# Reordering the delta network's convolution, and loading expert 0's weights before the router has chosen

## The chip, the cores and the metric

The kernel runs on one core of a Trainium2 chip. The metric is the device time of one execution in microseconds (us). A core has a matrix engine (TensorE, PE in the rows, with its weight loads as PEld), a vector engine (DVE), a scalar engine (ACT), a general engine (GpSimd, POOL) and a sync engine (SP), each with an instruction stream of its own that runs strictly in order. They wait for each other through semaphores. SP computes nothing; it issues most DMAs. SBUF is the on-chip memory, PSUM holds the matrix products in eight banks.

## The reference, cut to what matters

Two transformer blocks of depth 1 over 1024 tokens with 1024 features, one after the other, all in float32. Only the first block is touched by the change:

```python
h = modulate(rmsnorm(x, norm1_w), shift1, scale1)
r_q, r_k, r_v, r_g, d_q, d_k, d_v, d_z, d_a, d_b = split(h @ w_in)
ret = rmsnorm(retention(rotary(r_q), rotary(r_k), r_v)) * silu(r_g)
cq, ck, cv = split(silu(causal_dwconv(concat(d_q, d_k, d_v), conv_w)))   # 4 taps, 12 groups of 128 channels
dq, dk = l2norm(cq) * DN_HEAD_DIM ** -0.5, l2norm(ck)
beta, g = sigmoid(d_b), -exp(a_log) * softplus(d_a + dt_bias)
dn = rmsnorm(gated_delta_rule(dq, dk, cv, g, beta)) * silu(d_z)
x = x + gate1 * (concat(ret, dn) @ w_out)                                # the residual stage
h2 = modulate(rmsnorm(x, norm2_w), shift2, scale2)
# router: best of 4 groups, then best 2 of its 8 experts; 32 experts of 1024 -> 512 -> 1024
hid = silu(ragged_dot(xs, w1)) * ragged_dot(xs, w3)
x = x + gate2 * segment_sum(ragged_dot(hid, w2) * gate)
```

The second block (neighbourhood attention with a bias table `rpb`, gated linear attention, a 4096-wide MLP) reads the bias table that the convolution stage prepares on the side.

## The kernel before, in words

The program is a chain of stages, each ended by a barrier (`k.meet()`: every engine, SP too, announces itself and waits for the last one): `front` (modulation and the first projections), `retention`, `delta_conv`, `delta`, `residual`, `route`, `experts_pass`, and the second block's stages.

**The convolution stage** (`delta_conv`, 365 to 550 us) projects the 12 groups of channels in 6 pairs, `p` = 0 to 5. A pair is 7 steps of 4 matmuls (a Strassen-like scheme on sums of weights and sums of tokens). Step `n` writes a PSUM bank that step `n - 2` used, so it waits for what takes step `n - 2` out of the bank (`conv_taken`). Steps 0, 2, 3 and 6 are taken out by ACT (`conv_copy_scalar`, line 1380), steps 1, 4 and 5 by DVE (`conv_add_vector`, line 1462). After a pair, DVE applies the 4 taps (`conv_taps_vector`, lines 1479 and 1483), ACT the SiLU (line 1387), TensorE turns the channels into token rows between the steps of the next pair (`delta_conv_turn`, helper line 232), ACT and DVE take those out, and GpSimd scales them (`conv_rows_gpsimd`). Also on GpSimd: the sums of weights (`conv_weights_gpsimd` 1505 to 1511, `conv_last_weights_gpsimd` 1519), and the window mask that is added to the bias table of the second block (`near_bias_gpsimd`, line 1232, four adds of 128 x 960).

At the stage's start each stream does the gates too: TensorE turns `abT` (1289), DVE takes it out (1418), and ACT makes sigmoid, exp, abs, exp, ln (1338 to 1347) before it enters the pair loop. At its end, `delta_ahead` runs four steps of the delta stage's first tile on each engine before the barrier: on TensorE inside the last turn (1302), on GpSimd before the last group's rows (1545), on ACT and DVE after everything else.

**The residual stage** stores the rows of `x` and of its normed form `xn` from SP (1916, 1918), and SP waits for these stores before the barrier (1919 to 1921).

**The experts stage.** The router sorts 2048 token-expert pairs into blocks of up to 128 rows of one expert (or two half blocks of two experts, line 2526). `known` is the semaphore value that says the list of blocks is there. SP then loads weights, 6.3 MB for an expert as three DMAs of 2 MB (`experts_load`, 2427, 2428, 2435), into three sets of buffers in turn. A load into a set in use waits until TensorE is through with it. GpSimd gathers the blocks' token rows by indirect DMA (2462) once the tokens of each block are known. TensorE's first block waits for the first gather, the turned rows and the weights. With these inputs the router gives expert 0 84 of the 2048 pairs, and each expert with over 64 has a whole block of its own, so the first block is expert 0's.

## Time and profile before

| what | value |
|---|---|
| median of 3 runs | 3084.66 us (3079.02 to 3085.67) |
| the profiled execution | 3084.89 us, its span 3083.1 us |
| mean granted TensorE clock | 0.97 of full |
| TensorE busy | 2899.4 us (94%), 12002 matmuls |
| DVE, ACT, POOL busy | 39%, 20%, 23% |
| convolution stage, by the trace | 365 to 550 us |
| TensorE's first expert matmul, the last | 977.97 us, 1539 us |
| DMA | 415.12 MB, mean 135 GB/s; 403 to 426 GB/s from 1002 us to 1387 us |

The time is that of the whole program, and TensorE is busy for nearly all of it. What can be won is where TensorE waits. The profile's views give that by stage: the waits of one engine in a window, the instructions of each engine in order of time with the idle time ahead of them and what ended it, and the share of the DMA engines in short windows. A row's duration is of the whole merged group when it has "x" and a count. A busy share hides what matters here: two engines can be busy and slow each other down.

### The profile page before, as it was taken

The numbers are of one execution on the slowest core, as the hardware profiler recorded it, in microseconds if no ns is written. First come the engines' busy times: TensorE is split into PE (matmuls) and PEld (weight loads), VectorE is DVE, ScalarE is ACT, GpSimd is POOL, SyncE is SP. The second block draws the span as 40 slices with busy tenths as digits, with TensorE's granted clock in tenths as the row PEclk, the third lists the DMA queues.
The fourth block names the chain that finished last, engine by engine and source line by source line (L and its number), as shares of the span: only waits on it lengthen the run. The fifth ranks groups of instructions, "written<-read, shape, count | busy, mean of one in ns | idle before, by whom it ended". The sixth has DMA issues, their size and how long they took to land.

```text
span 3083.1 us, 30795 instructions
## 1 busy us (share of the span) xinstructions
PE 2899.4 (94%) x12002; PEld 1723.0 (56%) x12002; DVE 1209.6 (39%) x1999; ACT 629.7 (20%) x1351; POOL 714.1 (23%) x552
## 2 busy tenths in 40 slices
PE   7999899889897999999969999999999999999998
PEld 5786544788544666666634455557544444444443
DVE  6714766466213111111134134569734314133142
ACT  4001222322121221211222211147231000000001
POOL 3213455544121000000021000137521122111220
PEclk9999999899998999999989999999999999999999
DMA  8634486000216999999671100030201111111101
GB/s 263 221 55 51 92 193 171 1 28 28 90 77 269 403 426 425 426 426 407 269 257 62 55 1 14 14 106 1 85 32 55 41 41 41 41 55 42 41 28 55
DMA packets 180120, 415.12 MB, mean 135 GB/s; under 512 B 30644, under 2 KB 103796, under 8 KB 170872
## 3 DMA queue, kind: packets, MB, share of 16 engines
q1 hardware_dynamic: 163545, 370.52, 34.0%
q10 hardware_dynamic: 10512, 25.69, 2.6%
q0 software_dynamic: 5904, 16.78, 1.5%
q8 instruction: 100, 1.64, 0.2%
q14 instruction: 59, 0.48, 0.0%
HBM read 366.04 MB, written 59.88 MB: 138 GB/s over the span
## 4 chain that ended last, share of the span: by engine, by line
PE 87%; DVE 6%; issue 2%; DMA 2%; ACT 1%; POOL 1%; SPq 0%; DVEq 0%; ACTq 0%; POOLq 0%
PE bank L3760 27%; PE bank L2523 9%; PE bank L2526 8%; PE bank L2953 5%; PE bank L748 4%; PE bank L1267 4%; PE bank L1935 4%; PE bank L3127 3%; PE bank L232 3%; PE bank L3125 2%; PE bank L3459 2%; PE bank L883 2%; PE bank L3469 2%; PE bank L1838 1%; PE bank L1835 1%
## 5 line engine op out<-in xcount | busy, mean ns | idle before, releaser
L3760 PE MATMUL bank<-w_ff,uT 128*128 128x512 f32 x640 | 276.0, 592 | 0.0
L3760 PE MATMUL bank<-hT,w_ff 128*128 128x512 f32 x512 | 224.3, 596 | 4.3 <-DVE hT L3563 4.3
L3883 DVE TENSOR_TENSOR x_out<-x_out,bank 128x512 f32<-128x512 f32 x140 | 94.7, 687 | 291.5 <-PE bank L3760 291.3
L3760 PEld LDWEIGHTS bank<-w_ff,uT 128*128 128x128 f32 x640 | 121.6, 190 | 153.1 <-issue 153.1
L2523 PE MATMUL bank<-e_w,e_xsT 128*128 128x256 f32 x832 | 185.0, 383 | 1.6 <-DVE e_xsT L2609 1.6
L2526 PE MATMUL bank<-e_w,e_xsT 128*64 128x256 f32 x1408 | 159.3, 386 | 18.7 <-issue 18.7
L2523 PEld LDWEIGHTS bank<-e_w,e_xsT 128*128 128x128 f32 x832 | 158.6, 192 | 32.7 <-issue 11.3
L2953 PE MATMUL bank<-w_gla,nT 128*128 128x512 f32 x384 | 168.5, 599 | 1.3 <-ACT nT L2915 1.3
L3760 PEld LDWEIGHTS bank<-hT,w_ff 128*128 128x128 f32 x512 | 97.5, 191 | 126.3 <-issue 126.1
L3760 PE MATMUL bank<-h_sum,w_ff 128*128 128x512 f32 x384 | 166.1, 592 | 0.0
L2680 DVE TENSOR_TENSOR e_hid<-e_act,bank 128x256 f32<-128x256 f32 x48 | 20.2, 421 | 337.1 <-PE bank L2523 171.1
L2526 PEld LDWEIGHTS bank<-e_w,e_xsT 128*64 128x64 f32 x1408 | 113.1, 139 | 68.6 <-issue 30.2
L3824 POOL TENSOR_TENSOR w_ff<-w_ff,w_ff 128x2048 f32<-128x2048 f32 x9 | 42.7, 4749 | 355.7 <-PE bank L3760 352.5
L2953 PEld LDWEIGHTS bank<-w_gla,nT 128*128 128x128 f32 x384 | 73.2, 192 | 91.8 <-issue 89.4
L3760 PEld LDWEIGHTS bank<-h_sum,w_ff 128*128 128x128 f32 x384 | 73.0, 190 | 91.8 <-issue 91.8
L3797 ACT ACTIVATE uT<-bank 128x512 f32<-128x512 f32 x48 | 28.3, 600 | 468.9 <-PE bank L3760 468.9
L3870 DVE TENSOR_TENSOR uT<-uT,bank 128x512 f32<-128x512 f32 x48 | 33.1, 689 | 229.1 <-PE bank L3760 229.0
L3127 PE MATMUL bank<-nT,w_nqk 128*128 128x512 f32 x256 | 121.7, 605 | 0.0
L2462 POOL DMA_INDIRECT e_rows<-xn_rows,e_idx x25 | 25.0, 1001 | 405.1 <-PE bank L2492 402.6
L748 PE MATMUL bank<-w_in,hT 128*128 128x256 f32 x512 | 115.2, 383 | 0.0
L3444 POOL TENSOR_SCALAR n_sc<-n_sc,n_st 128x512 f32<-128x512 f32 x64 | 99.7, 1563 | 46.9 <-DVE n_st L3427 44.7
L3760 PE MATMUL bank<-w_ff,u_sum 128*128 128x512 f32 x256 | 110.5, 592 | 0.0
(534 smaller groups left out, 4932.9 us busy)
## 6 DMA issues: line engine op xcount, KB each, us to landing
e_w<-in_w SPq DMA_DIRECT2D x105, 2048.0 KB, 28.5
w_ff<-in_w_ff SPq DMA_DIRECT2D x32, 1024.0 KB, 5.3
y_rows<-zero SPq DMA_DIRECT2D x8, 3008.0 KB, 20.5
wa_rest<-in_w_ada SPq DMA_DIRECT2D x32, 512.0 KB, 6.0
y_rows<-e_y ACTq DMA_DIRECT2D x24, 512.0 KB, 10.1
wa<-in_w_ada SPq DMA_DIRECT2D x16, 512.0 KB, 11.0
w_qkv<-in_w_in SPq DMA_DIRECT2D x24, 256.0 KB, 8.4
w_gla<-in_w_in SPq DMA_DIRECT2D x3, 2048.0 KB, 20.3
```

The source lines that it names most:

```text
L232: t = k.nc.tensor.transpose(bank[:, h * P:(h + 1) * P], src[:, h * P:(h + 1) * P], k.c("ident"))
L748: t = pe.matmul(out, still[:, f, g * P:(g + 1) * P], moving[:, f, :], start=step in (0, 1, 3) and g % 2 == f == 0, stop=f == 3, skip_group ...
L883: t = pe.matmul(k.bank[6 + m % 2][:, :], hT[:, f, m * P:(m + 1) * P], wz[:, f, :], start=f == 0, stop=f == NK - 1)
L1267: t = pe.matmul(conv_bank(k, p, step)[:, :], weights[step][:, f, :], tokens[step](f), start=step in (0, 1, 3) and f == 0, stop=f == 3, ski ...
L1935: t = pe.matmul(k.bank[2 * (m % 2) + h][:, :], mixed, b.w[h][:, f, :], start=f == 0, stop=f == NK - 1)
L2523: return pe.matmul(out, xT, weights[0], start=start, stop=stop)
L2526: t = pe.matmul(out[tokens, :], xT[:, tokens], w, start=start, stop=stop)
L2953: t = pe.matmul(k.bank[3 * (i % 2) + j][:, :], b.nT[:, f, i * P:(i + 1) * P], b.w[at][:, f, :], start=f == 0, stop=f == NK - 1)
L3127: t = pe.matmul(bank[:, :], wqk[c // 2 % 2][:, f, c % 2 * P:(c % 2 + 1) * P], nT[:, f, h * BANK:(h + 1) * BANK], start=f == 0, stop=f == N ...
L3444: g.tensor_scalar(b.sc[n][:, :], b.sc[n][:, :], b.st[n][:, 2:3], None, ALU.mult).then_inc(*s.weights_ready.up().inc)
L3760: t = pe.matmul(bank[:, :], still, moving, start=step in (0, 1, 3) and f == 0, stop=f == 3, skip_group_check=True)
L3883: v.tensor_tensor(dst, dst, k.bank[4 * ((ph + step) % 2) + g][:, :], ALU.add).then_inc(*s.added.up().inc)
```

## The change

Five edits reorder the convolution stage, and one moves a load.

1. ACT's gate chain (sigmoid to ln) moves from before the pair loop to behind the copy of step 0 (`conv_gates_scalar`).
2. DVE's add of step 1 of pair 0 moves ahead of the gates.
3. GpSimd's four mask adds, once together behind group 2's rows, come one by one at the end of the rounds `p` = 1 to 4.
4. TensorE's four ahead steps move from inside the last turn to before the turns of the last two groups.
5. GpSimd's ahead steps move from before the last group to before the last two.
6. SP loads expert 0's three matrices into the set at 96 KB at the end of the residual stage, before its barrier. The sets are renumbered, so that this one is the first. After `known`, the first block's loads are skipped if its expert is 0 (a DMA with a condition), and done again otherwise.

```diff
-def near_bias_gpsimd(k, s, b):
+def near_bias_gpsimd(k, s, b, p):
...
-    for p in range(PAIRS):
-        b3 = b.bias[:, p, :].rearrange("p (r c) -> p r c", c=W)
-        g.tensor_tensor(b3, b3, wide(k.c("window"), 1, 2 * KH - 1), ALU.add).then_inc(*s.bias_ready.up().inc)
+    b3 = b.bias[:, p, :].rearrange("p (r c) -> p r c", c=W)
+    g.tensor_tensor(b3, b3, wide(k.c("window"), 1, 2 * KH - 1), ALU.add).then_inc(*s.bias_ready.up().inc)
@@ delta_conv_tensor
+    pe.wait_ge(*conv_taken(s, CONV_PAIRS - 2, 5))
+    pe.wait_ge(*conv_taken(s, CONV_PAIRS - 2, 6))
+    pe.wait_ge(*s.rows_ready(2 * RH))
+    delta_ahead(ahead)
     for j in (LAST_CHANNELS - 1, LAST_CHANNELS):
-        delta_conv_turn(k, s, b, j, ahead)
+        delta_conv_turn(k, s, b, j)
@@ delta_conv_scalar
-    a.wait_ge(*s.ab_taken(2))
-    a.activation(d.beta[:, :, :], b.ab[:, :, RH:], ACT.Sigmoid).then_inc(*s.beta_ready.up().inc)
...
         if p < CONV_PAIRS:
             conv_copy_scalar(k, s, b, p, 0)
+        if p == 0:
+            conv_gates_scalar(k, s, b, d)
@@ delta_conv_vector
     v.tensor_tensor(a21, a11, a21, ALU.subtract).then_inc(*s.x_summed.up().inc)
+    conv_add_vector(k, s, b, 0, 1)
     v.wait_ge(*s.ab_turned(1))
...
-        if p < CONV_PAIRS:
+        if 0 < p < CONV_PAIRS:
             conv_add_vector(k, s, b, p, 1)
@@ conv_rows_gpsimd
-        if j == 2:
-            near_bias_gpsimd(k, s, b)
...
-    if j == LAST_CHANNELS:
-        g.wait_ge(*conv_made(s, CONV_PAIRS - 1, 6))
-        g.wait_ge(*s.rows_ready(2 * RH))
-        g.wait_ge(*s.g_ready(1))
-        delta_ahead(ahead)
@@ delta_conv_gpsimd
+        if p == CONV_PAIRS:
+            g.wait_ge(*conv_made(s, CONV_PAIRS - 1, 6))
+            g.wait_ge(*s.rows_ready(2 * RH))
+            g.wait_ge(*s.g_ready(1))
+            delta_ahead(ahead)
         if p:
             for j in (2 * p - 2, 2 * p - 1):
-                conv_rows_gpsimd(k, s, b, dtok, d, j, ahead)
+                conv_rows_gpsimd(k, s, b, dtok, d, j)
+        if 1 <= p <= PAIRS:
+            near_bias_gpsimd(k, s, b, p - 1)
@@ residual_sync
         sy.wait_ge(*(s.xn_stored_0, s.xn_stored_1)[n](NT // 2))
+    for j in range(3):
+        experts_first_load(k, s, sets, j)
@@ experts_first_load, experts_sync, experts_load
+def experts_first_load(k, s, sets, j):
+
+    k.nc.sync.dma_start(sets[0][j][:, :, :], experts_source(k.io, j, slice(0, 1))).then_inc(*s.first_set_got.up().inc)
...
     sy.wait_ge(*known)
+    sy.wait_ge(*first_got)
     used = used_blocks(sy, experts)
...
+    if u == 0:
+        there = which[0] > 0
```

How the streams read before and after. First ACT at the start of the convolution stage (`abT` is the raw gates, `gates_u` and `alog` the gate chain, `conv_raw` the copies of steps 0, 2, 3). Before:

```order
L1336 ACTIVATE abT_120<-bank 8x512 x2
L1338 ACT_TABLE_LOAD
L1338 ACTIVATE beta_135<-ab_124 128x32
L1340 ACT_TABLE_LOAD
L1340 ACTIVATE alog_125<-alog_125 128x4
L1343 ACTIVATE gates_u_1_129<-gates_u_1_128 128x32
L1345 ACTIVATE gates_u_1_129<-gates_u_1_129 128x32
L1347 ACT_TABLE_LOAD
L1347 ACTIVATE gates_u_1_129<-gates_u_1_129 128x32
L1380 ACTIVATE conv_raw_1_116<-bank 128x512
L1380 ACTIVATE conv_raw_1_115<-bank 128x512 x2
```

After:

```order
L1334 ACTIVATE abT_120<-bank 8x512 x2
L1385 ACTIVATE conv_raw_1_116<-bank 128x512
L1367 ACT_TABLE_LOAD
L1367 ACTIVATE beta_135<-ab_124 128x32
L1369 ACT_TABLE_LOAD
L1369 ACTIVATE alog_125<-alog_125 128x4
L1372 ACTIVATE gates_u_1_129<-gates_u_1_128 128x32
L1374 ACTIVATE gates_u_1_129<-gates_u_1_129 128x32
L1376 ACT_TABLE_LOAD
L1376 ACTIVATE gates_u_1_129<-gates_u_1_129 128x32
L1385 ACTIVATE conv_raw_1_115<-bank 128x512 x2
```

The copy of step 0 is now ahead of the gates, the copies of steps 2 and 3 are still behind them.

GpSimd in the middle of the stage, from the scaling of group 2's rows on (`conv_ss` is the square sums of a group, `dtok` its rows). Before:

```order
L1536 TENSOR_TENSOR dtok_60<-dtok_60,conv_ss_123 128x8x128
L1232 TENSOR_TENSOR near_bias_131<-near_bias_131,consts_49 128x960 x4
L239 TENSOR_SCALAR conv_ss_123<-conv_ss_123 128x8
L241 TENSOR_TENSOR conv_ss_123<-conv_ss_123,consts_49 128x8
L1532 TENSOR_SCALAR conv_ss_123<-conv_ss_123 128x8
L1536 TENSOR_TENSOR dtok_60<-dtok_60,conv_ss_123 128x8x128
L1519 TENSOR_TENSOR w_qkv_1_1_105<-w_qkv_1_1_105,w_sum_1_109 128x512
```

After, the same stretch:

```order
L1542 TENSOR_TENSOR dtok_60<-dtok_60,conv_ss_123 128x8x128
L239 TENSOR_SCALAR conv_ss_123<-conv_ss_123 128x8
L241 TENSOR_TENSOR conv_ss_123<-conv_ss_123,consts_49 128x8
L1538 TENSOR_SCALAR conv_ss_123<-conv_ss_123 128x8
L1542 TENSOR_TENSOR dtok_60<-dtok_60,conv_ss_123 128x8x128
L1231 TENSOR_TENSOR near_bias_131<-near_bias_131,consts_49 128x960
L1525 TENSOR_TENSOR w_qkv_1_1_105<-w_qkv_1_1_105,w_sum_1_109 128x512
```

One of four mask adds is left here, behind both groups' rows.

TensorE at the end of the stage (`conv_out_1_117` is group 10, `conv_out_1_118` group 11; line 1797, later 1803, and the `dtok` turns are the ahead steps). Before:

```order
L1267 MATMUL bank<-hT_52,w_qkv_1_1_105 128x512 x4
L232 MATMUL bank<-consts_49,conv_out_1_117 128x128 x8
L232 MATMUL bank<-consts_49,conv_out_1_118 128x128 x4
L1797 MATMUL bank<-hT_52,consts_49 128x512
L232 MATMUL bank<-consts_49,dtok_60 128x128 x4
L232 MATMUL bank<-consts_49,conv_out_1_118 128x128 x4
L232 MATMUL bank<-consts_49,dtok_60 128x128 x4
```

After:

```order
L1266 MATMUL bank<-hT_52,w_qkv_1_1_105 128x512 x4
L1803 MATMUL bank<-hT_52,consts_49 128x512
L232 MATMUL bank<-consts_49,dtok_60 128x128 x4
L232 MATMUL bank<-consts_49,conv_out_1_117 128x128 x8
L232 MATMUL bank<-consts_49,conv_out_1_118 128x128 x8
L232 MATMUL bank<-consts_49,dtok_60 128x128 x4
```

The ahead steps stand before all turns of the last two groups.

## Rows read from the trace of the kernel before

**Rows 1.** TensorE's waits, 360 to 560 us: us in total, times, longest
```profile
PE bank L1267 <- ACT conv_raw L1380: 7.0, 1, 7.0
PE bank L1267 <- DVE conv_raw L1462: 4.1, 1, 4.1
```

**Rows 2.** Timeline, stage start: start, us, instruction, count [idle before]
```profile
369.85 3.70 PE L1267 MATMUL bank<-hT,w_qkv 128*128 128x512 f32 x8
380.51 9.25 PE L1267 MATMUL bank<-dtok,w_sum 128*128 128x512 f32 x16 [6.97 <-ACT conv_raw L1380]
396.47 10.46 PE L1267 MATMUL bank<-hT,w_qkv 128*128 128x512 f32 x24
...
372.50 3.35 DVE L1414 TENSOR_TENSOR hT<-hT 128x2048 f32<-128x2048 f32 x1
376.94 5.69 DVE L1425 TENSOR_TENSOR h_last<-hT,dtok 128x512 f32<-128x512 f32 x4
...
370.50 3.19 POOL L1511 TENSOR_TENSOR w_sum<-w_qkv,w_qkv 128x512 f32<-128x512 f32 x1
```

**Rows 3.** Timeline, middle of the stage: TensorE, DVE, GpSimd
```profile
467.31 5.09 PE L1267 MATMUL bank<-dtok,w_sum 128*128 128x512 f32 x8 [4.05 <-DVE conv_raw L1462]
494.58 3.60 PE L1267 MATMUL bank<-dtok,w_sum 128*128 128x512 f32 x8
...
397.46 0.75 DVE L1479 TENSOR_SCALAR conv_out<-conv_raw,conv_w 128x1024 f32<-128x1024 f32 x1
402.88 3.93 DVE L1483 SCALAR_TENSOR_TENSOR conv_out<-conv_raw,conv_w,conv_out 128x1024 f32<-128x1024 f32 x3
449.55 0.75 DVE L1479 TENSOR_SCALAR conv_out<-conv_raw,conv_w 128x1024 f32<-128x1024 f32 x1
466.48 0.68 DVE L1462 TENSOR_TENSOR conv_raw<-conv_raw,bank 128x512 f32<-128x512 f32 x1
481.04 0.75 DVE L1479 TENSOR_SCALAR conv_out<-conv_raw,conv_w 128x1024 f32<-128x1024 f32 x1
492.85 0.68 DVE L1462 TENSOR_TENSOR conv_raw<-conv_raw,bank 128x512 f32<-128x512 f32 x1
...
454.66 10.82 POOL L1232 TENSOR_TENSOR near_bias<-near_bias,consts 128x960 f32<-128x960 f32 x4
```

**Rows 4.** Timeline, end of the stage: TensorE, ACT, GpSimd
```profile
531.54 3.60 PE L1267 MATMUL bank<-hT,w_qkv 128*128 128x512 f32 x8
544.57 1.37 PE L1797 MATMUL bank<-hT,consts 128*128 128x512 f32 x2 [3.28 <-POOL hT L1756]
550.15 1.11 PE L232 MATMUL bank<-consts,dtok 128*128 128x128 f32 x4 [2.51 <-ACTq L164]
...
540.12 0.63 ACT L1387 ACTIVATE conv_out<-conv_out 128x512 f32<-128x512 f32 x1 [1.70 <-DVE conv_out L1483]
...
541.38 2.05 POOL L1549 TENSOR_TENSOR dtok<-dtok,beta 128x512 f32<-128x512 f32 x2 [13.85 <-ACT dtok L1394]
```

**Rows 5.** End of the residual stage: DVE, SP's last issue, SP's wait (us, times, longest)
```profile
924.24 1.37 DVE L1975 TENSOR_SCALAR hT<-bank,affine 128x128 f32<-128x128 f32 x4 [4.94 <-PE bank L232]
...
922.50 0.32 SPq L1918 DMA_DIRECT2D xn_rows<-xn_mixed  x1
...
SPq L1921 <- DMA xn_rows<-xn_mixed: 2.3, 1, 2.3
```

**Rows 6.** Experts: chain, SP issue, DMA windows (last: share, GB/s), TensorE's waits
```profile
963.87 10.89 DMA e_rows<-xn_rows,e_idx
...
994.36 0.33 SPq L2427 DMA_DIRECT2D e_w<-in_w  x1
...
1035.00:1040.00 5.00, 5.00 (x46) 3.38 (x42) 0.87 (x3) 0.84 (x3) 0.00 (x0) 1.00 0.79 268
1040.00:1045.00 5.00, 5.00 (x26) 1.72 (x24) 0.92 (x3) 1.55 (x5) 0.99 (x1) 1.00 0.86 350
...
PE bank L2526 <- issue: 18.7, 12, 2.9
```

More of the change, by code:

```diff
@@ L1290, in delta_gates_turn, with delta_conv_turn @@
     t.then_inc(*s.ab_turned.up().inc)
-def delta_conv_turn(k, s, b, j, ahead):
+def delta_conv_turn(k, s, b, j):
     pe = k.nc.tensor
@@ L1371, in delta_conv_scalar, with conv_gates_scalar @@
             conv_silu_scalar(k, s, b, LAST_CHANNELS, 0)
+def conv_gates_scalar(k, s, b, d):
+    a, A = k.nc.scalar, k.A
+    a.wait_ge(*s.ab_taken(2))
+    a.activation(d.beta[:, :, :], b.ab[:, :, RH:], ACT.Sigmoid).then_inc(*s.beta_ready.up().inc)
+    a.wait_ge(*s.a_log_loaded(1))
+    a.activation(b.alog[:, :], b.alog[:, :], ACT.Exp).then_inc(*s.neg_rate.up().inc)
+    a.wait_ge(*s.a_ready(1))
+    u = b.u1[:, :, :]
+    a.activation(u, b.u0[:, :, :], ACT.Abs).then_inc(*A.up().inc)
+    a.wait_ge(*A.now())
+    a.activation(u, u, ACT.Exp, scale=-1.0).then_inc(*A.up().inc)
+    a.wait_ge(*A.now())
+    a.activation(u, u, ACT.Ln, bias=1.0).then_inc(*s.soft_part.up().inc)
 def conv_copy_scalar(k, s, b, p, step):
@@ L1519, in conv_last_weights_gpsimd, with conv_rows_gpsimd @@
     g.tensor_tensor(b21, b21, b.wsum[1][:, :, :], ALU.subtract).then_inc(*s.w_summed.up().inc)
-def conv_rows_gpsimd(k, s, b, dtok, d, j, ahead):
+def conv_rows_gpsimd(k, s, b, dtok, d, j):
     g = k.nc.gpsimd
@@ L1903, in residual, with residual_sync @@
     k.meet()
-    k.retire(s)
-def residual_sync(k, s, b, x_out, xn_out, route_s, route_w):
+    k.retire([x for x in s if x is not s.first_set_got])
+def residual_sync(k, s, b, x_out, xn_out, route_s, route_w, sets):
     sy = k.nc.sync
@@ L2327, with experts_sets, experts_source, experts_pass @@
 UNIT_OF_LOAD = [u for u, (_, loads, _) in enumerate(UNITS) for _ in loads]
-def experts_pass(k, scale, shift, tokens, experts, known, xn, ys, indices, begin_next):
+def experts_sets(k):
     n_at = lambda kb: N_AT + kb * KB
-    sets = [[k.at(f"e_w{j}_{n}", n_at(48 * n + 16 * j), P, NK, DE) for j in range(2)] + [k.at(f"e_w2_{n}", n_at(48 * n + 32), P, DE // P, D)] for n in range(SETS)]
+    return [[k.at(f"e_w{j}_{n}", n_at(48 * n + 16 * j), P, NK, DE) for j in range(2)] + [k.at(f"e_w2_{n}", n_at(48 * n + 32), P, DE // P, D)] for n in (2, 0, 1)]
+def experts_source(io, j, e):
+    return io[("w1", "w3", "w2")[j]][e].squeeze(0).rearrange(("(p k) f -> p k f", "(p k) f -> p k f", "(k p) f -> p k f")[j], p=P)
+def experts_first_load(k, s, sets, j):
+    k.nc.sync.dma_start(sets[0][j][:, :, :], experts_source(k.io, j, slice(0, 1))).then_inc(*s.first_set_got.up().inc)
+def experts_pass(k, sets, first_got, scale, shift, tokens, experts, known, xn, ys, indices, begin_next):
+    n_at = lambda kb: N_AT + kb * KB
     b = Experts(*([w[j] for w in sets] for j in range(3)), [k.at(f"e_rows{n}", A_AT + 4 * n * KB, P, D) for n in range(ROWS_AHEAD)],
@@ L2340, in experts_pass @@
              "rows_got_0 rows_got_1 rows_got_2 rows_got_3 rows_got_4 rows_got_5")
-    experts_sync(k, s, b, experts, known)
+    experts_sync(k, s, b, experts, known, first_got)
     experts_gpsimd(k, s, b, tokens, experts, xn, indices)
```

33 lines of the change are left out of this document (10 added, 23 removed).

## The prediction

> **What bounds the kernel now.** I read the page first. TensorE is busy for 94% of the span, so only places where TensorE waits can give time, and a reordering pays exactly what it takes from them. Then I read TensorE's waits in the convolution stage: 7.0 us for an ACT copy and 4.1 us for a DVE add are the longest [rows 1], and at the stage's end 3.3 us for a GpSimd ahead step [rows 4]. Then the timelines of the engines around each of these waits [rows 2 to 4], to see what was late and what would be late next. Then the end of the residual stage, where SP gets new work ahead of a barrier [rows 5]. Last the experts stage [rows 6]: what the first block waits for, and whether a load that comes earlier is still earlier when TensorE waits for weights.
>
> **Start of the convolution (edits 1 and 2).** Steps 0 and 1 end at 369.85 + 3.70 = 373.55. Step 2 starts at 380.51, 6.97 us later, since ACT's copy of step 0 stands behind sigmoid to ln [rows 2]. These wait for DVE, whose last sum of tokens ends at 375.85 [rows 2]. With the copy ahead of the gates, step 2 needs only the GpSimd weight sum that ends at 373.69 [rows 2], so it starts at about 373.8. TensorE hardly stops, so it keeps its clock. Before, the 16 matmuls behind the wait took 9.25 us [rows 2] where two groups of 8 take 3.60 us each and overlap by 0.16 [rows 3], so 2.2 us were lost to a lower clock. Step 2 ends at 377.3.
>
> What is late next: step 3 needs DVE's add of step 1. That add now stands right behind the token sum, 375.85 + 0.7 = 376.6, in time; left behind the gates (before, it stood behind all of DVE's gate work) it would have taken the copy's place as the wait. Step 3 ends at 380.7. Step 4 needs ACT's copy of step 2, which is behind the gates. Their chain starts 0.7 us later than before because of DVE's moved add, and ends near 380.5, the copy near 381.1. That leaves a wait of 0.4 us. Step 5 needs DVE's four last token sums, before 376.94 to 382.63 [rows 2], now 0.7 later, 383.3, against a start of 384.6. Step 6 then starts at 388.1 instead of 396.47 [rows 2]. **Term: -8.4 us.** Ends: the copy of step 2 and the GpSimd sums of pair 1, which now run beside the taps, could take back 2 us (-6.4), and the whole wait with its clock is 9.2.
>
> The lead holds through the stage: TensorE has no other wait until 463 us. The DMAs of the later pairs' weights are issued when a pair's matmuls end and move with them.
>
> **Middle (edit 3).** In an ordinary round DVE needs from 481.04 to 492.85, 11.8 us, for the taps of two groups, and its add ends at 493.53. TensorE wants it at 494.58 [rows 3]. The slack is 1.05 us. With GpSimd still, the same taps took from 397.46 to 406.81, 9.35 us [rows 3]. In the round with the four mask adds (10.82 us on GpSimd) they took from 449.55 to 466.48, 16.9 us [rows 3]. Taking off half of an ordinary round's excess (1.2 us, one of the two row scalings lay in it) leaves 6.35 us for four adds, 1.6 us for each. TensorE waited 4.05 us and its next 8 matmuls took 5.09 instead of 3.60 [rows 3]: 5.5 us for this round.
>
> After the change every round from `p` = 2 to 5 meets one add, right behind the row scalings and so inside the taps. Each makes DVE 1.6 us longer, of which 1.05 is slack: 0.55 us for TensorE, four times, 2.2 us. **Term: -5.5 + 2.2 = -3.3 us.** If the adds cost nothing it is -5.5.
>
> The Trainium skill's page "SBUF — State Buffer", section "Who interferes with whom", speaks against this edit: a DVE instruction with two SBUF inputs and a GpSimd instruction that reads SBUF exclude each other for a whole instruction. By it each add costs DVE up to the add's whole length, 10.82 / 4 = 2.7 us, or 1.65 beyond the slack, four times 6.6 us, and the edit would lose 1.1 us instead of winning 3.3. The trace agrees with blocking as such, but with a smaller price (6.35 us for four), which I take. The sum by the page would be 3071.6 us.
>
> **End (edits 4 and 5).** Before, the ahead step on TensorE (line 1797) waited 3.28 us, until 544.57, for a GpSimd step that stood behind group 10's rows, and the last turns stood behind it [rows 4]. The next work came at 550.15, after the barrier. After: the last pair's matmuls end near 535.0 [rows 4], GpSimd's ahead product takes about 1 us, TensorE's ahead steps run 536.3 to 538.5, in the time in which it waited for group 10's SiLU. They are hidden. Group 11's last SiLU ends at 540.75 [rows 4], its turn near 541.8. Now GpSimd is the last: its scalings of groups 10 and 11 start at 541.38 and are four pieces at 2.05 us for two [rows 4], so 545.5. ACT and DVE are through at 544.3. The barrier opens near 545.5 instead of 550.15. **Term: -4.6 us.** Ends: -3.3 (the GpSimd wait alone goes) to -5.8 (ACT's end decides).
>
> **The early load (edit 6).** Two things.
>
> *The barrier.* SP's last store is issued at 922.50 + 0.32, and SP waits 2.3 us for it, until 925.1 [rows 5]. DVE ends at 925.61 and opens the barrier [rows 5]. Three more issues of 0.33 us with 0.1 between [rows 6] make SP ready at 926.4. **Term: +0.8 us.** No row shows whether an engine's arrival at a barrier waits for DMAs that it issued; if it does, see the slow rival.
>
> *The first block.* It waits for its rows: the gather, issued at 963.87, took 10.89 us [rows 6]. Its weights had been issued at 951 and landed in that time. The early load takes no wait away. The gather shares the DMA engines with the next blocks' weights: in the new kernel 5 loads of 2.1 MB are issued at 951, at some 420 GB/s that is work until 976 alone, so the gather has the same company. 0 us.
>
> *The later stalls.* TensorE waits 18.7 us in 12 pieces [rows 6], by the chain of waits all between 1161 and 1453 us, for weights: the DMA engines run at 425 GB/s there. A load that is out of the way early might help here. But only if the lead lives that long, and the buffers cap it. Before 994.36, when the first set comes free [rows 6], the old kernel had issued 8 loads and 7 gathers, 20.4 MB, work until about 999. The new one has issued 14.2 MB, work until 984, and then idles until 994. The lead in DMA work at that point is 5 us. At 1035 to 1045 the old kernel's DMA share falls to 0.79 and 0.86 [rows 6]: it has done all that was issued and waits for the next set to come free. The new kernel idles there too, only longer. From then on both are alike, and the stalls stay. 0 us.
>
> Nothing else moves. **Sum:** -8.4 - 3.3 - 4.6 + 0.8 = -15.5 us. The profiled execution took 3084.89 us (span 3083.1), 0.2 above the median of 3084.66, so 3084.9 - 15.5 = 3069.4, and I say 3069.
>
> **Rivals.**
> - *The lead survives.* Speaks for it: the DMA engines are the bound from 1161 to 1453. Against: the drained queue at 1037 [rows 6]. It would take the 5 us of lead off the 18.7 us of stalls: 3064. At most the whole 14.8 us of a 6.3 MB load: 3055.
> - *DVE becomes the bound of the rounds.* For: a slack of only 1.05 us [rows 3], which the mask adds and the GpSimd sums of pair 1 now use in every round. The price is the whole 5.5 us of the middle edit and 2 us of the first: 3069.4 + 3.3 + 2 = 3075. Against: the measured 1.6 us for each add.
> - *Slower: the barrier waits for the 6.3 MB.* Place: SP's arrival at the end of the residual stage. If it comes only when the load has landed, 6.3 MB at 425 GB/s is 14.8 us, with 2.3 us for the way there [rows 5] the barrier opens at 943.5, 17.8 us late. TensorE idles so long that it starts the router at the lower clock, another 2 us. That is 19.8 in the place of 0.8: 3088. It decides from a landing later than 941 us. Against: SP waits for its stores by explicit waits [rows 5], which would not be needed otherwise.
> - *The load isn't skipped.* If the first block were not expert 0's, set 0 would be loaded twice. The second load is hidden as it is now: 3069, with the old DMA picture. The router's result on these inputs speaks against it.
>
> **How the numbers follow.** Forecast 0.65; lead survives 0.12; DVE-bound rounds 0.12; barrier waits 0.07; not skipped 0.04. The likeliest gives 3069, its own range from the ends of the terms is 3065 to 3074. The range of 3061 to 3078 takes in most of the two neighbours and leaves out the barrier rival and the extreme of the lead. A measurement here can tell 0.2%, 6.2 us, from no change: faster is below 3078.5. All cases but the barrier are: 0.92. Within 0.2%: 0.05. Slower 0.03, where the barrier rival comes with less won in the convolution.
>
> **What would show it.** Right: TensorE's idle time before line 1266's second group below 1 us and no ACT release there; step 6 of pair 0 8 us earlier; waits of half a microsecond for DVE's add in rounds 2 to 5 instead of one of 4; last GpSimd scaling just before the barrier; DMA share near 0 from 984 to 994 us in old time and again before 1038, and 12 stalls of about 18.7 us as before. Wrong: the gather landing in much less than 10.9 us, stalls below 14 us, a barrier over 2 us later, or rounds that are longer than 27 us.

## The result and the profile after

The changed kernel takes 3058.45 us (median of 4, 3053.98 to 3060.79) against 3084.05 us: a ratio of 0.992, 95% interval 0.9904 to 0.9936, or 24.7 us (19.7 to 29.6). I forecast 15.5 us and a range down to 3061. The direction was right, the size too small. The profiled execution took 3056.61 us, span 3054.8, against 3083.1.

TensorE's waits in the convolution stage of the changed kernel, in the form of [rows 1]. The long waits for ACT's copy (7.0 us) and DVE's add (4.1 us) are gone:

```profile
PE bank L232 <- ACTq L164: 4.2, 1, 4.2
PE bank L1803 <- POOL hT L1762: 1.9, 1, 1.9
PE bank L1266 <- DVE conv_raw L1468: 1.3, 2, 0.9
```

The start of the stage, as [rows 2]:

```profile
365.82 3.70 PE L1266 MATMUL bank<-hT,w_qkv 128*128 128x512 f32 x8
369.72 7.13 PE L1266 MATMUL bank<-dtok,w_sum 128*128 128x512 f32 x16 [0.20 <-POOL w_sum L1517]
383.88 6.60 PE L1266 MATMUL bank<-hT,w_qkv 128*128 128x512 f32 x15
```

Step 2 waits 0.20 us instead of 6.97, its 16 matmuls take 7.13 instead of 9.25. From the barrier (361.84; 365.86 before) to step 6 it is 22.04 us instead of 30.61: 8.6 us less, 8.4 forecast.

The middle, as [rows 3]: DVE's adds, the waits on them, and two of the four mask adds:

```profile
425.29 3.67 PE L1266 MATMUL bank<-dtok,w_sum 128*128 128x512 f32 x8 [0.41 <-DVE conv_raw L1468]
451.15 3.60 PE L1266 MATMUL bank<-dtok,w_sum 128*128 128x512 f32 x8
...
411.18 0.75 DVE L1485 TENSOR_SCALAR conv_out<-conv_raw,conv_w 128x1024 f32<-128x1024 f32 x1
424.47 0.68 DVE L1468 TENSOR_TENSOR conv_raw<-conv_raw,bank 128x512 f32<-128x512 f32 x1
418.23 2.79 DVE L1489 SCALAR_TENSOR_TENSOR conv_out<-conv_raw,conv_w,conv_out 128x1024 f32<-128x1024 f32 x1
423.27 1.28 DVE L1489 SCALAR_TENSOR_TENSOR conv_out<-conv_raw,conv_w,conv_out 128x1024 f32<-128x1024 f32 x1
437.61 0.75 DVE L1485 TENSOR_SCALAR conv_out<-conv_raw,conv_w 128x1024 f32<-128x1024 f32 x1
448.39 0.68 DVE L1468 TENSOR_TENSOR conv_raw<-conv_raw,bank 128x512 f32<-128x512 f32 x1
...
417.61 2.33 POOL L1231 TENSOR_TENSOR near_bias<-near_bias,consts 128x960 f32<-128x960 f32 x1
450.19 1.88 POOL L1231 TENSOR_TENSOR near_bias<-near_bias,consts 128x960 f32<-128x960 f32 x1
```

The first mask add falls inside the taps: the four-tap pass of both groups takes 13.3 us (411.18 to 424.47), the one tap that runs beside the add 2.79 us where another takes 1.28, and TensorE waits 0.41. The second starts behind them, at 450.19, since GpSimd had waited 10 us for a weight load and came late to its rows. Those taps take 10.8 us and TensorE waits for nothing. The third add (476.09) falls behind the taps too, the fourth (499.11) inside, and there TensorE waits 0.9 us.

The end, as [rows 4]:

```profile
515.05 3.60 PE L1266 MATMUL bank<-hT,w_qkv 128*128 128x512 f32 x8
520.55 1.10 PE L1803 MATMUL bank<-hT,consts 128*128 128x512 f32 x2 [1.91 <-POOL hT L1762]
530.56 0.69 PE L232 MATMUL bank<-consts,dtok 128*128 128x128 f32 x2 [4.15 <-ACTq L164]
...
525.07 0.63 ACT L1392 ACTIVATE conv_out<-conv_out 128x512 f32<-128x512 f32 x1 [2.49 <-DVE conv_out L1489]
526.69 1.28 ACT L1721 ACT_TABLE_LOAD   x1
529.84 0.63 ACT L1724 ACTIVATE hT<-hT 128x512 f32<-128x512 f32 x1 [1.26 <-DVE hT L1654]
...
526.32 4.06 POOL L1548 TENSOR_TENSOR dtok<-dtok,beta 128x512 f32<-128x512 f32 x4 [3.94 <-ACT dtok L1399]
```

From the last group's start to the barrier's end: 15.5 us instead of 18.6, 3.1 less where I forecast 4.6. GpSimd's four scalings end at 530.38 and ACT's L1724 at 530.47. Both are last; the forecast had GpSimd alone. ACT's chain has a table load of 1.28 us in it.

The end of the residual stage, as [rows 5]: SP's last store, the three early issues, and TensorE behind the barrier:

```profile
900.51 0.32 SPq L1924 DMA_DIRECT2D xn_rows<-xn_mixed  x1
903.19 1.28 SPq L2351 DMA_DIRECT2D e_w<-in_w  x3
904.70 2.55 PE L2088 MATMUL bank<-hT,route_w 128*36 128x128 f32 x30 [2.48 <-SPq L164]
```

The stage is 1.07 us longer (128.12 against 127.05), 0.8 forecast. The experts stage, as [rows 6]: the gather in the chain of waits, block 0's issues passed by and the two sets behind them, DMA windows of 5 us, the stalls:

```profile
941.91 7.98 DMA e_rows<-xn_rows,e_idx
...
930.28 0.11 SPq L2453 DMA_DIRECT2D e_w<-in_w  x1
931.65 0.35 SPq L2453 DMA_DIRECT2D e_w<-in_w  x1
935.40 0.39 SPq L2454 DMA_DIRECT2D e_w<-in_w  x1
...
965.00:970.00 5.00, 5.00 (x25) 3.56 (x25) 1.79 (x5) 2.16 (x6) 0.99 (x1) 1.00 0.47 140
1010.00:1015.00 5.00, 5.00 (x35) 2.61 (x32) 1.79 (x5) 2.16 (x6) 0.99 (x1) 1.00 0.61 184
...
PE bank L2552 <- issue: 17.4, 12, 2.9
```

The load is passed by (0.11 instead of 0.36 us for an issue), the DMA engines run short of work before 967 and again near 1010 (share 0.47 and 0.61 in the two windows), and the 12 stalls are there, 17.4 us. The places are as forecast, the first stretch is shorter: the share is 0.79, 0.61 and 0.16 in the three windows of 2 us from 961 to 967, where ten microseconds near 0 were forecast. The gather is not as forecast: 7.98 us instead of 10.89.

Where the 28.3 us between the two spans are, stage by stage (starts of stages in each trace):

| stretch | before | after | change | forecast |
|---|---|---|---|---|
| front, unchanged code | 365.86 | 361.84 | -4.0 | 0 |
| convolution stage | 184.29 | 168.72 | -15.6 | -16.3 |
| delta stage, unchanged code | 248.51 | 246.02 | -2.5 | 0 |
| residual stage | 127.05 | 128.12 | +1.1 | +0.8 |
| router, barrier to first gather's issue | 38.16 | 37.21 | -0.95 | 0 |
| gather's issue to TensorE's first turn of rows | 10.94 | 8.03 | -2.9 | 0 |
| turns, then the first block | 19.34 | 16.82 | -2.5 | 0 |
| everything behind it | 2088.95 | 2088.04 | -0.9 | 0 |

Three questions follow. Are -4.0 and -2.5 scatter? What shortens the gather and the first block? Is the convolution's part right edit by edit?

### The profile page after: what moved, and what is told of

Same layout as the page of the kernel before. It is cut to its first block, busy times and chain, and to the rows that moved or that the text cites. A ratio compares the mean times of both kernels' runs of the same rounds, so it can differ in the third digit from the quotient of the medians.

```text
span 3054.8 us, 30798 instructions
## 1 busy us (share of the span) xinstructions
PE 2881.9 (94%) x12002; PEld 1709.3 (56%) x12002; DVE 1211.2 (40%) x1999; ACT 629.2 (21%) x1351; POOL 726.0 (24%) x552
## 4 chain that ended last, share of the span: by engine, by line
PE 86%; DVE 6%; DMA 2%; issue 2%; ACT 1%; POOL 1%; SPq 1%; POOLq 0%; ACTq 0%; DVEq 0%
PE bank L3786 27%; PE bank L2549 9%; PE bank L2552 8%; PE bank L2979 5%; PE bank L748 4%; PE bank L1943 4%; PE bank L1266 4%; PE bank L3153 3%; PE bank L232 3%; PE bank L3151 2%; PE bank L3485 2%; PE bank L883 2%; PE bank L3495 2%; PE bank L1844 1%; PE bank L1834 1%
## 5 line engine op out<-in xcount | busy, mean ns | idle before, releaser
L2552 PE MATMUL bank<-e_w,e_xsT 128*64 128x256 f32 x1408 | 160.5, 388 | 17.4 <-issue 17.4
L3823 ACT ACTIVATE uT<-bank 128x512 f32<-128x512 f32 x48 | 28.3, 600 | 468.8 <-PE bank L3786 468.8
```

The source lines that it names most:

```text
L2552: t = pe.matmul(out[tokens, :], xT[:, tokens], w, start=start, stop=stop)
```

## The experiments

Times of different experiments stand against runs of the kernel before on the same chip (pooled medians 3080.9 to 3082.6). From each trace I read the stages.

### The two halves, and what repeats

`conv_only` has edits 1 to 5, `load_only` has edit 6. 

> The kernel before with the five moves in the convolution alone, without the early load. Theory A (the early load is worth about 5 us more than I gave it: the first gather lands 3 us sooner and the first block runs at the full clock): the convolution stage takes 168.7 us as in the new kernel (15.6 less than before), the gather before the first block still takes about 10.9 us, the first block 17.4 us, and the time is 3068 to 3069. Theory B (the missing 10 us came with the convolution's moves, through the delta stage behind it or a clock that holds longer): 3061 to 3063, the delta stage at 246 us. Theory C (scatter between executions; the gather's length varies by itself): a gather of 8 us may show here too.

> The kernel before with expert 0's early load alone. Theory A: the residual stage 1.0 us longer, the gather 8.0 instead of 10.9 us, TensorE's first expert matmul 10.8 instead of 14.1 us behind the gather's issue, the first block 15.4 instead of 17.4 us at a granted clock near 1.0: about 4.5 us faster than before, 3079.5. The forecast on record: 0.8 us slower, 3085. Theory C: the gather anywhere from 8 to 11 us, without a bearing on the early load.

> The changed kernel once more, to see what repeats. Theory A: gather 8.0 and first block 15.4 us as in its first profile, delta stage 246 to 248.5 us; the 4 us that its first 180 us (unchanged code) were shorter do not have to repeat. Theory C: gather or first block come out near 10.9 and 17.4. Time 3054 to 3061 under each.

`conv_only`: 3063.49, ratio 0.9938 (0.9925 to 0.9951), 19.1 us. `load_only`: 3078.30, 0.9990 (0.9981 to 0.9999), 3.1 us. `after_again`: 3058.74, 0.9923 (0.9910 to 0.9936). In `conv_only` the gather takes 11.6 us to TensorE's first turn and the first block 15.7, in `load_only` 9.4 and 15.5, in `after_again` 7.8 and 14.1. So the early load does win, as theory A says, though alone it won less than the 4.5 us expected, since its gather was only 1.5 us shorter. `conv_only`'s time is 5 us below what A gave, which I had built on 3084. Its time lies nearer to theory B's 3061 to 3063, but its stages agree with A (convolution 167.6 us, delta stage 248.8, not B's 246), and the rest is put down to scatter, below.

> The kernel before once more, for its profile: how long its front stage is (365.9 us in the first profile, 360.5 to 363.5 us in five profiles of other kernels with the same front stage), its delta stage (248.5 us), its gather (10.9 us) and its first block. If the 365.9 was scatter, this one is near 362; if the changed code shortens the front stage in some way, near 366 again.

Its front takes 367.3 us, not 362: my guess of the value failed, and two profiles of the kernel before alone would look like an effect. But over all 17 profiles the front takes 359.3 to 367.3 us, and kernels with all five edits are among the long ones (`load_twice` below, 366.2) and kernels with few among the short ones (`before_hold`, 361.2). The delta stage takes 242.9 to 249.3 us, also without bearing on the edits: 244.6 to 249.3 in the eight with none or some of the convolution's edits, 242.9 to 248.8 in the nine with all five. So most of both differences is scatter between executions. On average the kernels with all five edits are 1.6 us shorter in the front and 1.3 us in the delta stage, each with a standard deviation of 1.8 to 2.6 us for a single profile, so a small effect there is neither shown nor excluded.

### Why the gather got shorter

These kernels change what is queued beside the gather. `load_twice` leaves block 0's usual load in place although the early load has been made, without these lines:

```diff
-    if u == 0:
-        there = which[0] > 0
```

`hold_rest` makes SP wait, before the third part of the next set and all loads behind it, until the first gather has landed. `before_hold` is the same in the kernel before, with `u == 0`:

```diff
+    if u == 1:
+        sy.wait_ge(*experts_rows_got(s)[0](1))
     for load, e in zip(loads, which):
```

> The changed kernel, but block 0's load is not passed by: expert 0's 6.3 MB are loaded early and once more at the usual place, so three sets are queued beside the first gather, as before. Theory A (the gather waits in the DMA engines for what is queued beside it): gather back at 10.9 us or more, the first block near 16 to 17 us, the residual stage still 1.1 us longer, about 5 to 6 us slower than the changed kernel: 3064. The 0.95 us that the router gained stays, if it comes from the later barrier. Theory B (the gain comes from something else in the early load, such as SP's work or where the barrier opens): time and gather as in the changed kernel, 3058.5.

> The changed kernel, with one wait more on the load queue: the third part of the second set's load and all loads behind it are issued only when the first gather has landed. If the gather's length is set by the loads that are queued beside it (theory A), it shrinks from 8.0 to 4 to 5 us, TensorE starts 3 to 4 us sooner, and the time is 3055 at the most for a median of 3058.5 of the changed kernel; the queue loses some 3 us of transfers, which the idle time behind 984 us takes in. If its length has nothing to do with them (theory C: it is the descriptors' own time), it stays 8 us and the time stays at 3058.

> The kernel before with one wait more: SP issues w2 of the first load and all of loads 1 and 2 only once the first gather has landed; no early load, no moves in the convolution. Theory A (contention): only 4.2 MB are queued ahead of the gather, and these have been issued 12.9 us earlier; the gather takes 5.5 us as when held in the changed kernel instead of 10.9, TensorE starts behind its warm-up matmuls, 3.6 us sooner, and the first block runs 2 us shorter at the full clock: 5.5 us faster than before, if w2 of the first block, issued at about 969.5, lands in time (2.1 MB at 420 GB/s is 5 us, first used about 985). Theory B: nothing gained, gather 10.9.

`load_twice`: 3065.22 us, 6.5 above the changed kernel (3064 expected), ratio to before 0.9952 (0.9939 to 0.9965). `hold_rest`: 3055.65, 0.9920 (0.9905 to 0.9934), about 3 us below the changed kernel and within its interval; its gather's rows landed sooner as expected, but TensorE started only 0.8 us sooner instead of 3 to 4. `before_hold`: 3083.26, 1.0005 (0.9996 to 1.0014). The stretches, in us; `load_ahead`, `tiny_early` and `warm3` are described further down. The fourth column is the moment, counted from the gather's issue, at which the loads' queue comes to the 16 KB packets of the next set, by the packet records of each trace:

| kernel | loads issued by the first gather | issue to first turn | first 16 KB packets | first block | block 2 to the mix stage's end |
|---|---|---|---|---|---|
| before | 7, an eighth under way | 10.9 | 3.8 | 16.2 | 1195.9 |
| before_again | same | 11.3 | 3.7 | 15.8 | 1191.5 |
| conv_only | same | 11.6 | 3.6 | 15.7 | 1195.6 |
| load_twice | 6, a seventh under way | 11.8 | 4.9 | 15.6 | 1195.8 |
| tiny_early | same | 13.2 | 4.8 | 16.5 | 1196.6 |
| load_ahead | 5 | 9.5 | 5.6 | 17.2 | 1193.5 |
| load_only | 5 | 9.4 | 6.7 | 15.5 | 1195.5 |
| after | 5 | 8.0 | 6.9 | 14.1 | 1195.1 |
| after_again | 5 | 7.8 | 7.1 | 14.1 | 1195.5 |
| warm3 | 5 | 8.9 | 7.4 | 17.0 | 1197.2 |
| hold_rest | 2, rest held | 7.2 | none beside it | 14.1 | 1196.1 |
| before_hold | 2, rest held | 7.2 | none beside it | 14.1 | 1206.0 |

The DMA queues in the first 7 us behind the gather's issue (the gather is on the software queue, the weights on the hardware queue; packets, MB, share of 16 engines). Kernel before:

```profile
q1 hardware_dynamic: 502, 2.81, 97.7%
q0 software_dynamic: 62, 0.19, 6.8%
```

Changed kernel:

```profile
q1 hardware_dynamic: 517, 2.45, 85.8%
q0 software_dynamic: 140, 0.36, 13.5%
```

The engines are nearly full in both, yet the gather's queue gets 6.8% of them in one and 13.5% in the other. `load_twice` has 7.9%, `conv_only` 6.2, `after_again` 13.9. So it is not the engines being busy that sets the gather's length. The obvious reading is the amount queued on them, but the packets speak for another one. In these traces `w1` and `w3` go in packets of 16 KB, of 0.61 us each (median), `w2` in packets of 4 KB, of 0.16 us, and so do the gathered rows (each queue also has packets of 4 bytes). The gather's queue has no packet in its first 4.4 us. From its first packet to TensorE's first turn of the rows, kernel before (968.30 to 974.81):

```profile
q1 hardware_dynamic: 164, 2.35, 84.2%
q0 software_dynamic: 162, 0.42, 16.1%
```

Changed kernel (946.37 to 949.94):

```profile
q1 hardware_dynamic: 212, 0.95, 66.7%
q0 software_dynamic: 187, 0.52, 37.2%
```

`load_ahead` (946.59 to 951.59), with the same five loads issued as the changed kernel:

```profile
q1 hardware_dynamic: 190, 1.68, 80.1%
q0 software_dynamic: 180, 0.49, 24.8%
```

The two queues move about one packet for one packet in all three. What differs is the packet that the gather's packets take turns with: 14 KB on average in the kernel before, where the loads' queue is already in `w1` and `w3` of the second set; 4.5 KB in the changed kernel, where it is still in `w2`; a mixture in `load_ahead`. The 16 KB packets of the next set begin 16.5 to 17.7 us behind SP's first load that moves data, in all 14 profiles without a hold, whatever is queued behind. The early load takes one set out and so moves that first load from 12.9 to 10.3 us ahead of the gather's issue, 1.3 us by the set that is passed by and 1.2 by the shorter router (next section but one). The gather's packets then fall into the 4 KB stretch. `load_twice` has only the second part (11.6 us), `load_ahead` only the first (11.5). So the gather goes by where the loads stand when its packets come (10.9 to 13.2 us with 16 KB packets from 3.6 to 4.9 us, 9.5 from 5.6, 7.8 to 9.4 from 6.7 to 7.4), and the amount queued behind them is not shown to matter. No kernel changed the size or the order of the packets alone, so this rests on the packets of these traces and not on an experiment of its own.

With the hold the loads' queue is empty when the gather's packets come, and they come 1.9 us behind the issue instead of 4.4 to 4.7. Why they come later beside loads is open.

SP's own rows show how far ahead the loads were issued. In the kernel before, the seventh load's issue takes 6.34 us instead of 0.35 (6.2 to 6.8 in all nine kernels with three sets queued), which would fit a queue with no room left; no run shows its depth:

```profile
954.17 0.40 SPq L2435 DMA_DIRECT2D e_w<-in_w  x1
956.53 6.34 SPq L2427 DMA_DIRECT2D e_w<-in_w  x1
962.97 2.34 SPq L2428 DMA_DIRECT2D e_w<-in_w  x1
963.87 1.28 POOL L2462 DMA_INDIRECT e_rows<-xn_rows,e_idx  x1 [0.91 <-POOL e_idx L2446]
```

`before_hold` shows the price of room made in another way. Its gather is short, TensorE starts the first block 4.3 us sooner and runs it 2.1 faster, and 10.1 us are lost again later, the stalls rising from 18.7 to 24.9 us. SP issued the third part of the first set 17.3 us behind its first part instead of 0.9, and all further sets behind that, in a stage that needs the DMA engines. Theory A's 5.5 us counted only whether the first block's own weights arrive. In `hold_rest` the same hold costs nothing that stands out of the scatter (1196.1 us in the last column, 1191.5 to 1197.2 in the kernels without a hold); there the early load had put the queue ahead.

### The clock in the first block

TensorE's windows from the gather's issue to the first turn, to the first block, and over the first block; the last three columns are granted clock, DMA share, GB/s. Kernel before:

```profile
963.87:974.81 10.94, 6.36 (x11) 2.50 (x11) 0.00 (x0) 0.00 (x0) 8.18 (x22) 0.79 1.03 427
974.81:977.97 3.16, 1.61 (x9) 1.24 (x9) 1.37 (x4) 2.35 (x5) 0.78 (x1) 0.58 1.01 429
977.97:994.15 16.18, 16.18 (x67) 13.90 (x67) 0.42 (x1) 1.20 (x3) 0.23 (x1) 0.87 1.02 420
```

Changed kernel:

```profile
949.94:952.66 2.72, 1.17 (x9) 1.00 (x9) 1.37 (x4) 1.95 (x5) 2.45 (x16) 1.00 1.05 446
952.66:966.76 14.10, 14.10 (x66) 12.40 (x67) 0.42 (x1) 1.60 (x3) 0.24 (x1) 1.00 0.82 339
```

TensorE has run its warm-up matmuls (until 971.2 before, 949.3 after) when it waits for the rows: 3.6 us before, 0.7 after. Behind the long wait it is partly at 1.2 GHz (0.58, then 0.87), behind the short one at 2.4 GHz throughout. That is the 2.1 us of the first block: the shorter gather pays twice. How much it pays the second time varies: behind waits of 2.1 us the block took 15.5 us in `load_only` (0.91) and 17.2 in `load_ahead` (0.82), behind 3.2 us 17.0 in `warm3` (0.83).

### The router's microsecond

The router gained 0.95 us in every kernel above with the early load. Two kernels separate the later barrier from the load:

```diff
 # tiny_early: one k row of each matrix is loaded early, the whole set at its usual place
-    ...dma_start(sets[0][j][:, :, :], experts_source(k.io, j, slice(0, 1)))
+    ...dma_start(sets[0][j][:, 0:1, :], experts_source(k.io, j, slice(0, 1))[:, 0:1, :])
 # load_ahead: the three experts_first_load calls ahead of sy.wait_ge(*s.x_stored(NT))
```

> The changed kernel, whose early load moves one eighth of the set or less (one k row of each matrix), while block 0's set is loaded whole at the usual place. SP issues three transfers ahead of the barrier as in the changed kernel, but three whole sets are queued beside the gather. If the router's 0.95 us come from the later barrier (TensorE's clock in the router is granted at another time), they show here too: residual stage 128.1, barrier to gather's issue 37.2 us instead of 38.2. If they come from the fact that SP issues no first load in the router, it is 38.2 here. Gather 11 to 11.8 us under each, time 3064 to 3065, as load_twice.

> The changed kernel with the three early issues ahead of SP's waits for its last stores instead of behind them. SP is through with the issues while the stores land. If the 6.3 MB do not slow the last stores' landing, the barrier is where it was in the kernel before (residual stage 127.05 instead of 128.1); if they do, later than in the changed kernel (a store that shares the DMA engines with them could take 5 us instead of 2.3: 130). For the router: 38.2 us if its 0.95 us come from the later barrier, 37.2 if they come from the load. Gather and first block as in the changed kernel. By the first, time as the changed kernel, 3058.5; with a slowed store 3060 to 3061.

`tiny_early`: residual stage 128.09 us, router 37.26; 3065.16 us. `load_ahead`: 127.15 and 38.22; 3060.02 us. Two expectations failed: the gather took 13.2 us in `tiny_early` (11 to 11.8 expected), and `load_ahead` did not keep the changed kernel's gather and first block (9.5 and 17.2 us, table above). So the router is shorter where the barrier is later, whatever is loaded. With the later barrier the first 16 matmuls of line 2118 (2110 before) take 1.98 us, at the full clock, and the other 16 take 3.65, where all 32 took 7.06, at the lower clock. Behind the same wait of 2.41 us the granted clock falls 31.7 us after the barrier instead of 29.2. That is 1.23 us, of which the router's earlier steps had lost 0.28. The barrier's 1.07 us come back as 0.95 from the clock's timing, so the edit costs 0.1 us there. In `load_ahead` the barrier opened as early as before, and the router was as long as before.

### The convolution, edit by edit

Each kernel is the kernel before with only the edits named (`gates_only` 1 and 2, `copy_only` 1, `bias_only` 3, `ahead_only` 4 and 5).

> The kernel before with edits 1 and 2 alone (ACT's gates behind the copy of step 0, DVE's add of step 1 ahead of its gates). On record for them: 8.4 us (6.4 to 9.2) in the convolution stage. From the changed kernel's trace: step 6 of pair 0 8.6 us sooner. If the lead stays through the stage, the kernel is 8.5 us faster. A rival: the long wait in round 2 (4.05 us for DVE) or the ahead step takes some of it back, 6 us or less.

> The kernel before with edit 1 alone: ACT's copy of step 0 ahead of its gates, DVE's add of step 1 still behind its gate work. On record: the add then takes the copy's place as the wait. In the trace of before DVE's gate work ends at 384.9 and the add at 385.6, against step 3's turn at 377.3: TensorE waits 8 us ahead of step 3 instead of 7 ahead of step 2, step 6 starts between 396 and 398 (396.47 before), and the kernel is 0 +/- 1 us from before, against 8.5 with both edits. The rival, that the copy alone carries the gain: 7 us or more faster.

> The kernel before with edit 3 alone, the four mask adds spread over four rounds. On record: 5.5 us gained in round 2 and 2.2 lost again in four rounds (1.6 us of DVE's time for each add, 1.05 of it slack), 3.3 us faster; by the longest blocking (2.7 us for each add) 1.1 us slower; with adds that fall beside nothing 5.5 us faster. The changed kernel's trace has two waits for DVE (0.4 and 0.9 us) and 3.9 us gained to the last group. In the convolution stage I expect 3.5 to 4.5 us.

> The kernel before with edits 4 and 5 alone, the ahead steps moved ahead of the last turns and rows. On record: 4.6 us (3.3 to 5.8). In the changed kernel ACT's chain (a table load of 1.3 us, the activation behind it, DVE's product) and GpSimd ended together 3.1 us sooner relative to the last group than before. Two of four profiles of kernels with the old end have a wait of 4.6 us for the GpSimd step instead of 3.3 and a stage 1.9 us longer, so 3.1 to 5.0 us in the convolution stage.

| kernel | convolution stage | against 185.3 | forecast | ratio of times (95%) |
|---|---|---|---|---|
| gates_only | 176.7 | -8.6 | -8.4 | 0.9978 (0.9968 to 0.9988) |
| copy_only | 187.8 | +2.5 | 0 | 1.0010 (1.0001 to 1.0019) |
| bias_only | 179.8 | -5.5 | -3.3 | 0.9987 (0.9978 to 0.9996) |
| ahead_only | 181.1 | -4.2 | -4.6 | 0.9985 (0.9976 to 0.9994) |
| all five | 168.1, mean of 9 | -17.2 | -16.3 | 0.9938 (0.9925 to 0.9951) |

The 185.3 is the mean of four profiles with the old convolution (184.29, 184.43, 186.19, 186.33; the wait for the GpSimd ahead step is 3.3 or 4.6 us in them). With the new one nine profiles lie between 167.5 and 168.8. So a single profile with the old end can be off by 1 us: the same wait is 4.1 us in `gates_only`, 3.6 in `copy_only` and 4.6 in `bias_only`.

`copy_only` shows the pairing of edits 1 and 2. TensorE's timeline in it:

```profile
372.30 3.70 PE L1267 MATMUL bank<-dtok,w_sum 128*128 128x512 f32 x8 [0.20 <-POOL w_sum L1512]
384.31 6.53 PE L1267 MATMUL bank<-dtok,w_sum 128*128 128x512 f32 x8 [8.30 <-DVE conv_raw L1463]
```

The wait moves from step 2 to step 3, from ACT's copy to DVE's add, and grows from 6.97 to 8.30 us, and the clock falls behind it as before (6.53 us for 8 matmuls instead of 3.60). Edit 1 alone makes the kernel 3 us slower (0.3 to 5.9).

### A shorter warm-up, with and without the hold

In `hold_rest` SP, released by the rows, issued the held load 5.4 us behind the gather's issue, but TensorE was in its warm-up until 7.2. `hold_warm3` shortens that; `warm3` has the shorter warm-up without the hold:

```diff
-    keep_warm(k, 5, 6)
+    keep_warm(k, 3, 6)
```

> The changed kernel with the hold of hold_rest and three warm-up matmuls instead of five between the router and the first block. With the hold the first rows landed some 5.4 us behind their issue, but TensorE was busy with its warm-up until 7.2 us behind it. Each warm-up is 1.28 us at the lower and 0.85 us at the higher clock. If the clock stays up over the shorter warm-up, the first block starts 1.5 to 2 us sooner: 3053.5 to 3054. If two warm-ups less leave TensorE at the lower clock, the first block is 2 us longer again and nothing is won: 3056.

> The changed kernel with three warm-up matmuls instead of five and no hold. The gather takes 7.9 us in the changed kernel and TensorE waits 0.4 to 0.7 us for it behind its warm-up; with two warm-ups less it waits 2.2 us longer for the same landing. So nothing is won: 3058.5, and 2 us are lost at the first block (3060.5) if the clock falls in the longer wait. If the shorter warm-up itself gave hold_warm3's gain, it is 3053 or less.

`hold_warm3`: 3050.02 us (3047.91 to 3057.48), ratio 0.9904 (0.9891 to 0.9918). `warm3`: 3060.54, ratio 0.9929 (0.9915 to 0.9942), the changed kernel's within the scatter. The windows of `hold_warm3`, from the gather's issue:

```profile
938.00:943.43 5.43, 4.45 (x7) 1.92 (x8) 0.00 (x0) 0.00 (x0) 4.26 (x4) 0.58 0.71 228
943.43:946.03 2.60, 1.05 (x10) 0.89 (x8) 1.37 (x4) 1.95 (x5) 2.25 (x5) 1.00 0.83 259
946.03:960.13 14.10, 14.10 (x66) 12.40 (x67) 0.42 (x1) 1.61 (x3) 2.71 (x16) 1.00 1.02 407
```

The rows are turned 5.4 us behind the issue, 2.5 sooner than in the changed kernel, with no wait, at the full clock. In `warm3` the wait for the rows is 3.2 us, the turns run at 0.50 of the clock and the first block takes 17.0 us. Neither part shows a gain clear of the scatter alone. The stage accounts for about 2.5 us. The median is 8.4 to 8.7 below the changed kernel's, and its interval touches that kernel's (0.9904 to 0.9936), so its place ahead of the kernel before is certain, and ahead of the changed kernel likely, by 2 to 3 us, more than that not shown.

## Why the prediction was right and wrong

**Start (-8.4): right.** 8.6 us in the trace and 8.6 in `gates_only`'s stage. That DVE's add would take the copy's place without edit 2 was right too; I did not foresee that it would be worse than before.

**Middle (-3.3): right in kind, too small alone.** 3.9 us in the changed kernel, 5.5 in `bias_only`, which has one wait of 0.4 us for DVE left. I charged four adds inside the taps. Only two fall inside in the changed kernel and one in `bias_only`, because GpSimd comes late to its rows after waiting for weights. The price for one inside was about right: 1.5 us for the tap beside the first add (2.79 instead of 1.28), 1.6 in my sum. The sum with 2.7 us for each of four adds, by which the edit would have lost 1.1 us, is refuted. The rule of the Trainium skill behind it ("SBUF — State Buffer", "Who interferes with whom") is not: that tap began 0.6 us behind the start of the add and took 1.5 us longer, about as long as the add still ran (1.7 us). It says what two instructions do that overlap, not how many will. My total by the page was also added up wrong: with +1.1 in the place of -3.3 it is 3073.8 us, not 3071.6.

**End (-4.6): right in kind, 1.5 too large.** 3.1 us in the changed kernel, 4.2 in `ahead_only` against the mean. I let GpSimd's ahead products take 1 us; beside DVE's taps they took 1.7 and 2.0, and the last taps and ACT's SiLU came 1.4 us later. ACT's table load and chain ended with GpSimd. In the first profile the convolution's sum (-15.6 for -16.3) is nearer than this term, since the start and the middle gave 0.8 us more than I had.

**Barrier (+0.8): right in size (1.07), and given back** by the router's clock, which I had not looked for.

**First block (0): the step that failed.** I wrote that the gather "has the same company", since 5 loads of 2.1 MB keep the engines busy for its whole length. That treated a busy DMA engine as one state. The engines were busy in both kernels, but not with the same packets: the gather's packets take turns with the loads' one for one, with 16 KB packets of 0.61 us in the kernel before (162 to 164) and with 4 KB packets of 0.16 us in the changed one, since the loads now start 10.3 us ahead of the gather instead of 12.9. `load_twice` brings the long gather back, `load_ahead` half of it. I also left out what a longer or shorter wait does to the clock of the first block. It is 2.9 us of gather, 0.4 of turns and 2.1 of first block, 5.4 together; `load_twice` gives 6.5 in time. The early load's gain here is luck of timing in part: nothing in the edit aims at the gather. In the profile of `load_ahead`, whose loads start 1.2 us further ahead of it, these three stretches take 29.3 us together (9.5, 2.7 and 17.2), against 24.9 in the changed kernel and 30.3 before. Theory C, that the gather varies by itself, falls: kernels with three sets queued have 10.9 to 13.2 us, with two sets 7.8 to 9.5, without overlap.

**Later stalls (0): right.** 18.7 to 17.4 us. Of the other kernels without the hold eight have 16.8 to 17.6 and four 20.5 to 22.1, in both groups some with and some without the load. The lead is lost in the two stretches in which the DMA engines run short of work, as forecast. `before_hold` and `hold_rest` add what I missed: the lead is no gain by itself, but it can be spent on a pause of the load queue.

So -15.5 becomes -15.5 - 5.4 - 0.7 (barrier) - 0.9 (convolution) = -22.5, within the measured interval of 19.7 to 29.6. The remaining 2 us and the 4.0 us of the front I put down to scatter: I started from a profile and a median of three runs (3084.66) that were 2 to 4 us above the pooled medians of 17 to 27 runs.

What stays open is why the gather's first packet comes 4.4 us behind its issue beside loads and 1.9 without them, and what moves the 16 KB packets by some tenths of a microsecond between kernels with the same loads: in `load_only` they begin 0.2 to 0.4 us sooner than in the two profiles of the changed kernel, and its gather is 1.4 to 1.6 us longer.

## What to carry to other kernels

Before you write "hidden" or "same company" for a small transfer on TensorE's path, look at the packets and not only at the busy share. Take each queue's packets and MB in the small transfer's own window: if they come one for one, the small transfer's time is its packets times what a packet beside it costs, and that depends on which bulk load is in turn when it comes. An untested idea that follows from it is to put the load with the small packets beside the gather by order and not by chance. A wait that ends warm-up work costs twice, in itself and in the clock behind it, so fit the warm-up's length to the landing. And take the base of a forecast of a few tenths of a per cent from many runs, and compare stages and not spans.

## What I had not expected of the hardware

- With the DMA engines about full in both cases, the gather's packets and the loads' moved one for one, and the gather's share went by the size of the loads' packets: 162 to 164 packets and 16.1% of the engines beside 14 KB packets (kernel before), 187 to 212 and 37.2% beside 4.5 KB packets (changed kernel), each from the gather's first packet to the first turn. The Trainium skill ("DMA: Bandwidth & Descriptors", "Queues, rings and completion order") has each DMA engine take turns between queue rows packet by packet. The traces agree with it, by these counts.
- A barrier that opened 1.07 us later made the router 0.95 us shorter, in all eight profiles with the late barrier (37.2 to 37.3 us against 38.2 in the nine others), by when TensorE's clock fell.
- Stretches of unchanged code differed by 8.0 us (front) and 6.4 us (delta stage) between executions, while the total time of the kernel before spread by 6 to 10 us within one chip's runs.
